# Mixer products of a hybrid recurrent trunk: full-precision operands replaced by three products of split operands

## What is computed

```python
def swiglu(x, wg, wu, wd):
    return (jax.nn.silu(x @ wg) * (x @ wu)) @ wd

def token_mix(u, l, P, lb_l, ...):
    proj = u @ P['w_in'][l]                       # 1024 -> 7936 columns
    pa, pb, pc, pg = jnp.split(proj, [...], axis=-1)
    oa, ... = rwkv7_mixer(pa, ...)                # 8 heads x 64, state update
    ob, ... = rglru_mixer(pb, ...)                # convolution, gates, scan
    oc, ... = hgrn2_mixer(pc, ...)                # 4 heads x 128
    ga, gb, gc = jnp.split(jax.nn.sigmoid(pg), 3, axis=-1)
    merged = ga * (oa @ P['proj_a'][l]) + gb * (ob @ P['proj_b'][l]) + gc * (oc @ P['proj_c'][l])
    return merged @ P['w_out'][l], ...

for l in range(DEPTH):
    x = x + 0.5 * rmsnorm(swiglu(rmsnorm(x, g1), ...), ...)
    x = x + rmsnorm(token_mix(rmsnorm(x, gm), ...), ...)
    x = x + 0.5 * rmsnorm(swiglu(rmsnorm(x, g2), ...), ...)
```

## Time and profile before

| | us |
|---|---|
| median of 3 runs | 2304.16 (2302.93 to 2304.97) |
| the profiled execution, device time | 2305.04 |
| its span, first to last instruction | 2303.3 |
| PE busy | 2158.8 (94%) |
| DVE busy | 1142.7 (50%) |
| ACT busy | 663.1 (29%) |
| DMA engines, q1 | 28.5% |

### The profile page before, as it was taken

The page is one execution under the profiler, slowest core; times in us unless marked ns, Lnnn a source line. Parts: engine busy times, 40 slices in busy tenths (PEclk is TensorE's granted clock), DMA queues, the critical chain, the costliest instruction groups (busy, mean ns, idle before and its releaser), DMA issues.

```text
span 2303.3 us, 29512 instructions
## 1 busy us (share of the span) xinstructions
PE 2158.8 (94%) x11960; PEld 1811.7 (79%) x11960; DVE 1142.7 (50%) x1787; ACT 663.1 (29%) x751; POOL 36.0 (2%) x72
## 2 busy tenths in 40 slices
PE   5999899999999997999979997999999999979997
PEld 4999767777766665999979996677776666669996
DVE  4443435676566523444264534266755664254443
ACT  3433322122132203443344332212212421034432
POOL 0000000000000000000000000000000000000000
PEclk9999999999999998999989999999999999989998
DMA  4444231111122233344434442211112222324442
GB/s 170 153 146 165 92 110 61 65 48 64 61 86 110 103 110 110 136 156 146 147 117 158 146 165 83 100 61 47 65 65 79 91 98 99 122 92 160 148 155 87
DMA packets 37049, 251.98 MB, mean 109 GB/s; under 512 B 4609, under 2 KB 4673, under 8 KB 8161
## 3 DMA queue, kind: packets, MB, share of 16 engines
q1 hardware_dynamic: 32112, 234.60, 28.5%
q0 software_dynamic: 4848, 16.13, 1.9%
HBM read 242.05 MB, written 8.67 MB: 109 GB/s over the span
## 4 chain that ended last, share of the span: by engine, by line
PE 83%; DVE 9%; ACT 3%; DVEq 3%; DMA 1%; issue 1%; SPq 0%; ACTq 0%
PE dps L465 40%; PE dps L402 15%; PE dps L419 12%; DVE tmp L983 2%; PE mx L556 2%; PE mx L550 2%; PE mx L558 2%; PE mx L432 1%; ACT tmp L753 1%; DMA raw<-in_wstream 1%; DVE x L986 1%; ACT L753 1%; PE mx L664 1%; PE mx L674 1%; DVEq L1379 1%
## 5 line engine op out<-in xcount | busy, mean ns | idle before, releaser
L980 DVE TENSOR_TENSOR wlo<-raw,whi 128x2048 fp32r<-128x2048 f32 x136 | 311.4, 2292 | 396.7 <-ACT whi L753 389.3
L465 PE MATMUL dps<-uh,whi 128*128 128x320 f32 x1408 | 430.0, 305 | 26.7 <-DVE ul L980 26.7
L465 PE MATMUL dps<-uh,wlo 128*128 128x320 f32 x1408 | 436.4, 310 | 0.0
L465 PE MATMUL dps<-ul,whi 128*128 128x320 f32 x1408 | 435.1, 309 | 0.0
L419 PE MATMUL dps<-u,raw 128*128 128x320 f32 x1280 | 409.1, 446 | 0.0
L753 ACT ACTIVATE whi<-raw 128x2048 fp32r<-128x2048 f32 x136 | 259.8, 1912 | 327.4 <-PE dps L465 325.0
L465 PEld LDWEIGHTS dps<-uh,whi 128*128 128x128 f32 x1408 | 266.7, 189 | 29.2 <-issue 28.6
L419 PEld LDWEIGHTS dps<-u,raw 128*128 128x128 f32 x1280 | 227.7, 194 | 70.6 <-issue 12.9
L465 PEld LDWEIGHTS dps<-uh,wlo 128*128 128x128 f32 x1408 | 266.9, 190 | 0.0
L465 PEld LDWEIGHTS dps<-ul,whi 128*128 128x128 f32 x1408 | 266.1, 189 | 0.0
L465 PE MATMUL dps<-hfh,whi 128*128 128x320 f32 x704 | 221.1, 314 | 0.0
(11 more groups left out here) (249 smaller groups left out, 2229.2 us busy)
## 6 DMA issues: line engine op xcount, KB each, us to landing
raw<-in_wstream SPq DMA_DIRECT2D x220, 1024.0 KB, 4.8
hs<-in_st_hgrn POOLq DMA_DIRECT2D x8, 512.0 KB, 3.5
out_o_hgrn<-hsn POOLq DMA_DIRECT2D x8, 512.0 KB, 2.9
sw<-in_smallw POOLq DMA_DIRECT2D x2, 1024.0 KB, 8.5
ss<-in_st_rwkv POOLq DMA_DIRECT2D x8, 256.0 KB, 3.9
out_o_rwkv<-ssn POOLq DMA_DIRECT2D x8, 256.0 KB, 2.3
x<-in_xT SPq DMA_DIRECT2D x1, 1280.0 KB, 6.1
out_yT<-x SPq DMA_DIRECT2D x1, 1280.0 KB, 4.5
```

The lines of the kernel that those rows point to most:

```text
L465: m = pe.matmul(dps[:, 2 * half + c, 0:T], w[:, k, c * P:(c + 1) * P], v[:, k0 + k, :], start=first and k == 0 and i == 0, stop=last and k ...
L980: return nc.vector.tensor_tensor(out, a, b, op)
```

## The change

The mixer's products take split operands too. The normalised input becomes `nh` and `nl` (`nh` in the room of `u`, `nl` in that of `x`; x itself is written to memory in the meantime, into the output tensor, and read back before the mixer's last addition). The branch outputs and `merged` are split into room that is free by then. Weights are split by halves: 82 halves h a layer. ACT makes the high part of a half (`high`) in one of six rooms `HOMES[h]`, which is free once PE has finished the half that had it before (`BEFORE[h]`); DVE makes the low part (`low_half`) in place, over the raw weights. So a buffer of `raw` is used until both halves have been multiplied. The calls of `high` and `low_half` are written by hand into the lists of ACT and DVE. Core of the diff:

```diff
+def half_homes():
+    first = [("A", 0), ("A", 1), ("C", 0), ("C", 1)]
+    last = [("B", 0), ("B", 1), ("A", 0), ("A", 1)]
...
+        if h < H_TURN + 12:
+            homes.append(first[h % 4])
+        elif h < H_G0 + 4:
+            homes.append(("A", h % 2))
+        elif h < H_PROJ:
+            homes.append(("B", h % 2))
...
-                        sp.wait_ge(S["block_done"], l * NBLK + (j + 1))
+                        wait_half(sp, l, last_half(j - 2))
                     load(l, 0, order[j - B_A] - s, s)
+                    if j == B_A + 1:
+                        sp.wait_ge(S["x_new"], l * 12 + 8)
+                        sp.dma_start(yT, x[:, :, :]).then_inc(S["x_spilled"], 16)
...
+            def product(m_out, h, k, src, first, last):
+                wh, wl = high_half(h), whole_half(rlo, h)
+                hi, lo_ = src
+                for i, (w, v) in enumerate(((wh, hi), (wh, lo_), (wl, hi))):
+                    m = pe.matmul(m_out[0], w[:, k, m_out[1]:m_out[1] + P], v[:, k, :], start=first and i == 0,
+                                  stop=last and i == 2, skip_group_check=True)
...
+            def high(l, h):
+                j, c = half_block(h)
+                if c == 0:
+                    act.wait_ge(w_loaded[j % 2], (l * (NBLK // 2) + j // 2) * 16 + 16)
+                if BEFORE[h] is not None:
+                    act.wait_ge(S["half_done"], l * NHALF + (BEFORE[h] + 1))
...
+                fn(high_half(h), whole_half(raw, h), ACT.Copy).then_inc(S["half_hi"], 1)
...
+            def low_half(l, h):
+                dve.wait_ge(S["half_hi"], l * NHALF + (h + 1))
+                tt(whole_half(rlo, h), whole_half(raw, h), high_half(h).bitcast(F32), ALU.subtract)\
+                    .then_inc(S["half_lo"], 1)
...
                         prepare(l, p + 1, li)
+                    if p and li in (3, 5):
+                        low_half(l, h0 + 2 + li // 4)
                     dve.wait_ge(S["pt_done"], n * 5 + li)
...
+                    if c == 1:
+                        low_half(l, h0 + 4)
...
+                for h in range(H_PROJ, H_OUT):
+                    br, i, part = (h - H_PROJ) // 4, (h - H_PROJ) % 4, h % 2
+                    k = slice(2 * i, 2 * i + 2)
+                    wait_half(dve, l, h)
+                    dst = merged[:, k, :] if br == 0 else xs[:, 0:2, :]
+                    m = mul(dst, dps[:, 2 * part:2 * part + 2, 0:T], gate[:, 8 * br + 2 * i:8 * br + 2 * i + 2, :])
+                    m.then_inc(pair_free[part], 1)
...
+                    low_half(l, h + 4)
```

More of the change, by code:

```diff
@@ L145, in trunk @@
         rs = sb("rs", T)
-        raw = [sb(f"raw{i}", BLK) for i in range(2)]
-        sw = sb("sw", 4, 512)
+        raw, rlo = zip(*[shared(f"raw{i}", BLK, views=[(f"rlo{i}", (BLK,))]) for i in range(2)])
+        sw, whb = shared("sw", 4, 512, views=[("whb", (BLK,))])
         prm_all = sb("prm_all", L, NPARAM)
@@ L718, in _ @@
                     rwkv_pair(l, p, p < HP - 1)
-                dense(l, B_G0, Q_G0, 1)
+                for h in range(H_G0, H_G0 + 4, 2):
+                    one_block(l, h)
                 pe.wait_ge(S["xc_ready"], l + 1)
@@ new lines, in _ @@
+                for h in range(H_OUT, NHALF):
+                    j, c = half_block(h)
+                    half_in(l, h, Q_OUT + j - B_OUT)
+                    for k in range(KD):
+                        if h == H_OUT and k % 2 == 0:
+                            pe.wait_ge(S["merged_lo"], l * 4 + (k // 2 + 1))
+                        m = product((dps[:, 2 * (j % 2) + c, 0:T], 0), h, k, (merged_hi, merged_lo), k == 0, k == KD - 1)
+                    m.then_inc(S["half_done"], 1)
+                    if c and j > B_OUT:
+                        norm_sum(l, 3, (j - B_OUT - 1,))
@@ L855, in rwkv_pair @@
                         key_norm(n + 1)
+                high(l, h0 + 4)
                 if more:
@@ L896, in _ @@
                 norm(l, 2)
+                for j in range(4):
+                    act.wait_ge(S["nf_ready"], l * 4 + (j + 1))
+                    fn(nh[:, 2 * j:2 * j + 2, :], ho[:, 2 * j:2 * j + 2, :], ACT.Copy).then_inc(S["nh_ready"], 1)
+                for h in range(2, 4):
+                    high(l, h)
                 fn(spc[:, 0, :], pcol("lru_lam", 0, 4), ACT.Abs)
@@ L905, in _ @@
                 act.drain().then_inc(S["pl_ready"], 1)
+                for h in range(4, 6):
+                    high(l, h)
                 act.wait_ge(S["lora_in_ready"], l + 1)
@@ L914, in read_a @@
                     read_pair(l, B_A + 2 + i, s, pa[:, t:t + 2, :], ACT.Copy).then_inc(pair_free[s], 1)
+                    if i == 2 or i == 5:
+                        act.drain().then_inc(S["pa_ready"], 1)
+                    for h in range(6 + 2 * i, 8 + 2 * i):
+                        high(l, h)
                 def read_low_rank(kind):
@@ L947, in _ @@
                 act.wait_ge(S["shift_out_ready"], l + 1)
-                for s in range(2):
-                    read_pair(l, B_G0 + s, s, gate[:, 2 * s:2 * s + 2, :], ACT.Sigmoid).then_inc(pair_free[s], 1)
+                high(l, H_G0 + 2)
+                read_pair(l, B_G0, 0, gate[:, 0:2, :], ACT.Sigmoid).then_inc(pair_free[0], 1)
+                high(l, H_G0 + 3)
+                high(l, H_G0 + 4)
+                read_pair(l, B_G0 + 1, 1, gate[:, 2:4, :], ACT.Sigmoid).then_inc(pair_free[1], 1)
                 for kind in range(2):
@@ L1084, in ffn @@
                     split_lo(0, KF + j, j % 2)
+                if f == 0:
+                    for h in range(2):
+                        low_half(l, h)
                 norm_out(l, 4 * f + 1, names[1], 0.5)
@@ L1434, in _ @@
                 token_shift(l, pa, 12, 2, None).then_inc(S["lora_in_ready"], 1)
+                for h in range(4, 10):
+                    low_half(l, h)
                 dve.wait_ge(S["pa_ready"], l * 2 + 1)
@@ L1471, in _ @@
+                low_merged(3)
+                for h in range(H_OUT + 4, NHALF):
+                    low_half(l, h)
                 norm_out(l, 3, "mix_post_g", 1.0)
```

348 lines of the change are left out of this document (231 added, 117 removed).

## The result

The changed kernel takes 2468.0 us (median of 4 runs, 2466.6 to 2471.0) against 2304.4 before: 1.071 times as long, 95% interval 1.069 to 1.073. The prediction was 2438, in a range of 2350 to 2500. The profiled span grew from 2303.3 to 2466.4 us, and the mean granted clock fell from 0.976 to 0.937.

What follows compares the result with a forecast made beforehand. PE was taken to bound the projection, and DVE, ACT and PE in turn the pairs; the profiled span 2303.3 plus 94 of waits plus 40 of clock gives 2437, so 2438 us, range 2350 to 2500.

Steps and rivals of the forecast that it cites:

- the heads: HGRN heads: -3.6 us a layer in all, a window of 32 us becoming 31.1.
- the walk through the lists: Stage by stage delays from what stands behind each new instruction in the in-order lists: 46.9 us a layer, 94 in all.
- the clock: Falls to 0.50 after PE waits, 1.7 us each; 12 of 14 priced, 20 us a layer, 40 in all.
- part A: Start of the mixer: +7.1 us a layer, all PE gains there (104 products) lost in waits for reloads and lists.
- fourth pair, RG-LRU: Up to the first HGRN head: +11.1 us, from low and high parts ahead of gates, exponentials and head functions.
- projection, output: Projection +12.7 us from turns of 11.5 us a block, low part blocking the multiplication; output +1.7 from later low part and reloads.
- The ceiling of 129: Most the change can give, where PE sets the pace: 656 products a layer from 0.538 to 0.440 us.
- second and third pair: +7.45 us each: level 3 and level 5 products wait for low parts on DVE, level 5's subtraction moving by 3.95.
- (a): Whole kernel: waits as forecast, but the clock holds or its falls lie off the path: 2398 us; chance 0.15.
- (b): Buffers turn without blocking, dense stretches taking 7.2 instead of 8.6 us a block: -14 a layer, 2276 us; chance 0.09.
- (c): PE sets the pace everywhere, so shorter products are worth nearly all: 2180 us; chance 0.03.
- (d): Pairs and before the heads: half the low parts' delays fall into waits, half the clock's cost: 2389 us; chance 0.18.

Runs made afterwards that it cites:

- filler: Changed kernel with 24 more matmuls in each of the projection's 6 blocks, where PE otherwise waits: 2466.4 us against 2468.0.
- the run above: Kernel before, with split products in the projection and output alone and loads by halves: 2283.3 us, 0.991 of before.
- level 5 order: Changed kernel with level 5's low part ahead of the preparation on VectorE: 2477.1 us; with 11 matmuls more a pair in the remaining wait: 2462.6 us.
- VectorE's order changed: Changed kernel with the low part of half h+2, not h+4, after the multiplication of half h in the projection: 2402.7 us.
- every wait attacked: Changed kernel plus reload by halves, high part first, low part h+3 in projection, level 5 order, earlier part A loads and ACT reads: 2340.4 us.
- the pairs without their low parts: Kernel with every wait attacked, seven eighths of the low part left out for 24 halves a layer: 2306.5 us against 2340.4.
- the reload by halves: Changed kernel with each half of a buffer loaded by its own 512 KB DMA once PE is done with that half: 2395.9 us.

## Why the prediction was nearly right

The forecast was 30 us short of the result, with the direction right, and the places too but for the heads, which became longer and not shorter. Over the whole program the walk through the lists gave 94 us and the rest without the clock is 83 (198 of waits less 115 of work); the clock gave 80 for 40. So the walk erred high, the clock low, and the two misses cancel in part. Layer 0, prediction beside measurement; the measured lengthening is taken apart by the clock loss (after less before, from the 1 us windows):

| term | predicted without clock | measured | of it clock | rest |
|---|---|---|---|---|
| part A | +7.1 | +13.9 | 7.8 | +6.1 |
| first pair | +3.0 | +2.1 | 0.1 | +2.0 |
| second pair | +7.45 | +10.6 | 3.4 | +7.2 |
| third pair | +7.45 | +9.1 | 1.6 | +7.5 |
| fourth pair, RG-LRU | +11.1 | +11.9 | 3.7 | +8.2 |
| heads | -3.6 | +1.9 | 5.1 | -3.2 |
| projection, output | +14.4 | +27.6 | 14.8 | +12.8 |
| sum | 46.9 | 77.1 | 36.5 | 40.6 |

Part A counts 1.6 us by which its first product came later; from that product on it is 12.3 longer.

- **Price of a product, low and high part.** 0.440 predicted; 48 matmuls, 16 products, take 7.04 to 7.3 us with f32r, 0.440 to 0.457 a product, and 0.443 in the run above. The prediction read 0.440 for 0.538 as three passes for four; it is 0.82, not three quarters, and no run shows what makes the rest. Low part 1.22 measured for 1.21, high part 1.05 for 1.03. The ceiling of 129: 115 arrived as less work.
- **The walk through the lists** holds within 3 us a stage, and errs high by 6 a layer, half of it in RG-LRU. The turn of the projection was to be 11.5 us without the clock (its terms add to 11.4); it is 11.85 with the clock held (filler) and 13.95 without.
- **Part A** had one wait that I took too short. Half 2 started at 305.57 and not 303.2: I counted reload, high and low part, but the last to come was ACT's reading of half 0's sums, which stands behind two high parts and two table loads. The waits for PE in the first 88 us of the mixer:

```profile
PE dps L467 <- ACT ov L831: 6.9, 1, 6.9
PE dps L467 <- DVE nl L1124: 5.6, 1, 5.6
PE mx L581 <- DVE E L1127: 3.4, 1, 3.4
```

- **The clock is the term that was mis-sized**: 20 a layer predicted, 36.5 measured in layer 0; in the whole program 80 for 40. Both factors were low. I priced 12 waits a layer; stretches below a clock of 0.9 went from 19 to 53 in the program, 17 more a layer. And I took 1.7 us for each from the one fall of rows 9; the added ones cost 2.4 on average, since some lasted longer: in four of the projection's five turns the clock was low for some 7 us, ahead of the output and in part A of layer 1 for up to 10. By place, at 1.7 each, the 14 waits gave part A 3.4, the second and third pair 3.4, the stretch before the heads 3.4, projection and output 13.6, the heads nothing (the places named add to 16 with level 3, which was left out as too short). The table has 7.8, 5.0, 3.7, 14.8 and 5.1. So the projection was priced about right, and the shortfall lies in part A, in the heads, where three falls were added that I hadn't foreseen, and in the discount from 14 to 12. In the projection every turn fell anew, as the Trainium skill's section on the oscillation of the clock in real kernels says of such a pattern ("TensorE: Matmul & The Clock Gate", section "HAM oscillation — how this bites in real kernels"); this case's trace agrees in each of the five turns. Beyond the changed kernel's own profile, the runs show stretches of 17 to 27 us in a pair.
- **Rivals.** (a), a clock that costs nothing, falls: the level 5 order with and without filler differs by 14.5 us for more work. (b), buffers that turn without blocking, isn't this kernel, but it is nearly the one with VectorE's order changed: the block there takes 7.3 us, as (b) has it. Yet the total with every wait attacked stays at 2340, not 2276: its pairs with the RG-LRU are 31 us longer than before in layer 0, where (b) had 13, and it loses 83 us of work to the clock for 34 before, where (b) had no such loss. (c), TensorE's pace everywhere, falls: 58 of 193 us. (d) put half of the low parts' delays into waits; the second and third pair have 7.2 and 7.5 of the 7.45 us, so nearly all of it was on the path, and the pairs without their low parts are 3.7 shorter.
- **The spill of x** shows no cost, as said, though no run left it out: the reload of weights beside the read back took 4.84 us like the others; the read back takes 8.2 us in the page's row against 4.5 for the write, and lies under the projection.

What stays open: what decides whether the clock comes back after 3.4 us or after 27 from the same wait in the same code. One such stretch made a pair some 7 or 8 us longer, so a gain of that size is read from its stage and not from the total.

## What to carry to other kernels

A cheaper matmul that asks other engines for work in return paid only in the stages where the matmuls were the bound and those engines had room: here in the projection and the output, and there it gained 17 us, where the change over the whole mixer lost 164. Before spreading such a split, write down for each in-order list what stands behind the new instruction; one line put two places later was worth 65 us. And when a wait is shortened, look at the clock behind it: a fix can be right and measure slower.

## What the runs showed of the hardware

- The same wait in the same code is not always followed by the same stretch at a granted clock of 0.50. Behind 3.86 us at level 5 of a pair it was 3.4 us in the changed kernel, and 27 in one pair each of the kernels with the filler and with the reload by halves. Behind 1.73 us ahead of the state chain it was none, 17 or 20.5 us. PE is busy throughout the long ones (26.00 of 26 us). With eleven matmuls in place of the second wait no stretch longer than 10.3 us was left in the pairs of two kernels.
- A DMA of 512 KB into 128 partitions took 3.8 us, one of 1 MB 4.8 (medians of 160 and 140). Half the size saves a fifth.
- 24 matmuls in an otherwise idle place lowered the time of their turn by 2.1 us: added work on TensorE can cost less than nothing.
